# Streaming-encoder trunk on one core: x loaded in four pieces, the first weight slot in two halves, the second slot's low part made on VectorE

## The reference, cut to what matters

```python
def rmsnorm(x, g):
    xf = x.astype(jnp.float32)
    y = xf * lax.rsqrt(jnp.mean(xf * xf, axis=-1, keepdims=True) + EPS)
    return (y * g.astype(jnp.float32)).astype(x.dtype)

def stick_breaking_mixer(h, w_in, w_out):      # layer 0; w_in is 2048 x 6144
    qkv = h @ w_in
    q, k, v = jnp.split(qkv, 3, axis=-1)
    ...
    return o @ w_out

def reference(x, ...):
    for i in range(DEPTH):
        h = rmsnorm(x, norm_mix[i])
        x = x + (stick_breaking_mixer if i == 0 else mlstm_mixer)(h, ...)
        x = x + hierarchical_moe(rmsnorm(x, norm_ffn[i]), ...)
    return rmsnorm(x, norm_final)
```

## Time and profile before

| what | value |
|---|---|
| median of 3 runs | 1786.22 us (1786.12 to 1786.3) |
| the profiled execution | 1786.37 us, span 1784.6 us from first to last instruction |
| mean granted TensorE clock | 0.946 |
| TensorE busy | 1570.1 us, 88% of the span |
| VectorE busy | 731.6 us, 41% |
| ScalarE busy | 423.9 us, 24% |
| GpSimd busy | 57.7 us, 3% |
| moved by DMA | 543.79 MB, mean 305 GB/s |

### The profile page before, as it was taken

One profiled execution on the slowest core, in us unless ns is written; L12 is line 12 of the kernel. 1 busy time (PEld: TensorE's weight loads), 2 busy tenths in 40 slices (PEclk: granted clock), 3 DMA queues, 4 the chain that ended last, 5 costly groups with the idle time before them and its releaser, 6 DMA issues.

```text
span 1784.6 us, 25622 instructions
## 1 busy us (share of the span) xinstructions
PE 1570.1 (88%) x9901; PEld 1070.3 (60%) x9901; DVE 731.6 (41%) x1143; ACT 423.9 (24%) x571; POOL 57.7 (3%) x82
## 2 busy tenths in 40 slices
PE   7999999999987788778799999999998877887785
PEld 7999999887433233323287988988863333233331
DVE  4544444444322223222264756657443322222233
ACT  5344343433000000000154334334320000000002
POOL 4010000100000000000011000000000000000000
PEclk9999999999998899889899999999999998899887
DMA  8545455458999999999954465555689999999996
GB/s 270 189 146 181 148 182 166 144 212 313 394 424 425 427 424 425 425 428 424 411 170 141 144 209 168 164 194 175 225 345 426 424 425 425 427 424 425 425 427 268
DMA packets 149419, 543.79 MB, mean 305 GB/s; under 512 B 8736, under 2 KB 25456, under 8 KB 116208
## 3 DMA queue, kind: packets, MB, share of 16 engines
q1 hardware_dynamic: 148448, 541.14, 78.1%
q0 software_dynamic: 912, 1.82, 0.4%
HBM read 540.83 MB, written 2.10 MB: 304 GB/s over the span
## 4 chain that ended last, share of the span: by engine, by line
PE 58%; DMA 29%; SPq 6%; DVE 2%; ACT 2%; issue 1%; DVEq 0%; ACTq 0%
PE psum_G L663 32%; DMA ring<-in_moe_w 29%; PE psum_S L663 16%; SPq L508 6%; PE psum_A L663 6%; PE psum_T L663 3%; DVE w_lo L407 1%; ACT w_hi L403 1%; ACT h L1313 0%; DMA x<-in_x 0%; PE psum_A L670 0%; ACT squares L1147 0%; DVE x L1658 0%; DVE h L1904 0%; PE psum_T L899 0%
## 5 line engine op out<-in xcount | busy, mean ns | idle before, releaser
L663 PE MATMUL psum_A<-ring,arena 128*32 128x512 f32 x1984 | 298.5, 731 | 155.6 <-DMA ring<-in_moe_w 153.9
L407 DVE TENSOR_TENSOR w_lo<-ring,w_hi 128x2048 fp32r<-128x2048 f32 x126 | 289.2, 2298 | 289.2 <-ACT w_hi L403 285.0
L403 ACT CAST w_hi<-ring 128x2048 fp32r<-128x2048 f32 x128 | 244.2, 1908 | 244.6 <-PE psum_G L663 155.8
L663 PEld LDWEIGHTS psum_A<-ring,arena 128*32 128x32 f32 x1984 | 68.1, 122 | 331.9 <-issue 331.6
L1787 DVE COPY arena_two<-psum_A 128x512 f32<-128x512 f32 x64 | 44.3, 692 | 365.8 <-PE psum_A L663 365.4
L1817 DVE TENSOR_TENSOR x<-x,psum_S 128x512 f32<-128x512 f32 x128 | 88.0, 687 | 173.8 <-PE psum_S L663 173.8
L663 PE MATMUL psum_G<-xT_hi,w_hi 128*128 128x256 f32 x512 | 148.8, 291 | 1.1 <-DVE w_lo L407 1.1
L663 PE MATMUL psum_G<-xT_hi,w_lo 128*128 128x256 f32 x512 | 144.7, 283 | 0.0
L663 PE MATMUL psum_G<-xT_lo,w_hi 128*128 128x256 f32 x512 | 144.7, 283 | 0.0
L663 PE MATMUL psum_G<-ring,arena_two 128*32 128x512 f32 x1024 | 121.0, 614 | 22.9 <-DMA ring<-in_moe_w 22.9
L1329 ACT ACTIVATE arena<-psum_T 128x64 f32<-128x64 f32 x64 | 14.3, 224 | 500.0 <-PE psum_T L663 500.0
(11 more groups left out here) (243 smaller groups left out, 2116.3 us busy)
## 6 DMA issues: line engine op xcount, KB each, us to landing
ring<-in_moe_w SPq DMA_DIRECT2D x376, 1024.0 KB, 19.7
ring<-in_sb_w_in SPq DMA_DIRECT2D x48, 1024.0 KB, 5.1
ring<-in_ml_w_in SPq DMA_DIRECT2D x48, 1024.0 KB, 5.1
ring<-in_sb_w_out SPq DMA_DIRECT2D x16, 1024.0 KB, 4.9
ring<-in_ml_w_out SPq DMA_DIRECT2D x16, 1024.0 KB, 5.1
extra_one<-in_moe_w SPq DMA_DIRECT2D x4, 1024.0 KB, 8.6
extra_two<-in_moe_w SPq DMA_DIRECT2D x4, 1024.0 KB, 17.6
x<-in_x SPq DMA_DIRECT2D x2, 1024.0 KB, 6.0
```

Of the source, the lines that this page charges most:

```text
L403: act.copy(w_hi[:, slot_place(j), :], ring[:, slot_place(j), :]).then_inc(hi_made, 1)
L407: dve.tensor_tensor(w_lo[:, slot_place(j), :], ring[:, slot_place(j), :], w_hi[:, slot_place(j), :].bitcast(F32), ALU.subtract).then_inc(l ...
L663: return pe.matmul(dst, lhsT, rhs, start=start, stop=stop, skip_group_check=True)
```

## The change

- x comes in four loads of 512 KB: first the columns 0 to 1023 of both token blocks, then the columns 1024 to 2047 of both. TensorE waits for the first two before unit 0, and for the other two before unit 4.
- Slot 0 comes in two loads of 512 KB (k-tiles 0 and 1, then 2 and 3), with a semaphore for each half. ScalarE casts and VectorE subtracts each half by itself. TensorE starts on the first half, and waits for the second (`lo_made` 1) ahead of k-tile 2.
- The split of slot 0 moves behind unit 3 (it was behind unit 1) on ScalarE and VectorE. ScalarE casts slot 1 behind unit 4 (it was unit 3).
- In layer 0 VectorE makes the low part of slot 1, behind its unit 5, and counts it. GpSimd's split of slot 1 and the waits for it (`pool_lo_made`, the drain) are gone from layer 0; GpSimd goes from its constants straight to `load_small`. Layer 1 stays as it was.

```diff
-        x_loaded = [sem(f"x_loaded_{b}") for b in range(TB)]
+        x_loaded = [sem(f"x_loaded_{n}") for n in range(2)]
+        first_half_loaded = sem("first_half_loaded")
+        first_half_hi = sem("first_half_hi")
+        first_half_lo = sem("first_half_lo")
...
+        def first_slot(tensor, half):
+            return tensor[:, slot_place(0), half * (SLOT // 2):(half + 1) * (SLOT // 2)]
+
+        def first_slot_hi(act):
+            act.wait_ge(first_half_loaded, 16)
+            act.copy(first_slot(w_hi, 0), first_slot(ring, 0)).then_inc(first_half_hi, 1)
+            act.wait_ge(raw_loaded[0], 16)
+            act.copy(first_slot(w_hi, 1), first_slot(ring, 1)).then_inc(hi_made, 1)
+
+        def first_slot_lo(dve):
+            dve.wait_ge(first_half_hi, 1)
+            dve.tensor_tensor(first_slot(w_lo, 0), first_slot(ring, 0), first_slot(w_hi, 0).bitcast(F32),
+                              ALU.subtract).then_inc(first_half_lo, 1)
+            dve.wait_ge(hi_made, 1)
+            dve.tensor_tensor(first_slot(w_lo, 1), first_slot(ring, 1), first_slot(w_hi, 1).bitcast(F32),
+                              ALU.subtract).then_inc(lo_made, 1)
...
-            for b in range(TB):
-                sp_eng.dma_start(x[:, b, :], x_in[0, b * P:(b + 1) * P, :]).then_inc(x_loaded[b], 16)
+            for n in range(2):
+                for b in range(TB):
+                    c = slice(n * D // 2, (n + 1) * D // 2)
+                    sp_eng.dma_start(x[:, b, c], x_in[0, b * P:(b + 1) * P, c]).then_inc(x_loaded[n], 16)
+            for half in range(2):
+                sp_eng.dma_start(first_slot(ring, half).rearrange("p (k n) -> p k n", k=2),
+                                 sb_w_in[0].rearrange("(k p) n -> p k n", p=P)[:, 2 * half:2 * half + 2, 0:COLS]
+                                 ).then_inc(raw_loaded[0] if half else first_half_loaded, 16)
             for layer in (0, 1):
                 if layer == 0:
-                    mix_stream(layer, 0, range(RAW))
+                    mix_stream(layer, 0, range(1, RAW))
...
-            split_lo_one(0)
             load_small(0)
...
                 for u in range(KT // 2):
+                    if layer == 0 and u % 4 == 0:
+                        pe.wait_ge(x_loaded[u // 4], 16 * TB)
...
-                    pe.wait_ge(lo_made, mix_slot(layer, i, j) + 1)
+                    if layer == 0 and isinstance(i, int) and i == 0 and j == 0:
+                        pe.wait_ge(first_half_lo, 1)
+                    else:
+                        pe.wait_ge(lo_made, mix_slot(layer, i, j) + 1)
...
+                                    if j == 0 and kk == 2:
+                                        pe.wait_ge(lo_made, 1)
...
-                else:
-                    for b in range(TB):
-                        pe.wait_ge(x_loaded[b], 16)
...
-                    if u == 3 or (u == 1 and layer == 0):
-                        split_hi(act, layer, 0, u // 2)
+                    if layer == 0 and u == 3:
+                        first_slot_hi(act)
+                    if u == (3 if layer else 4):
+                        split_hi(act, layer, 0, 1)
...
-                    if u == 1 and layer == 0:
-                        split_lo(dve, layer, 0, 0)
-
-                dve.wait_ge(pool_lo_made, layer + 1)
-                dve.drain().then_inc(lo_made, 1)
+                    if layer == 0 and u == 3:
+                        first_slot_lo(dve)
+                    if layer == 0 and u == 5:
+                        split_lo(dve, layer, 0, 1)
+
+                if layer:
+                    dve.wait_ge(pool_lo_made, 1)
+                    dve.drain().then_inc(lo_made, 1)
```

## The result

The changed kernel takes 1791.4 us (median of 9 runs, 1790.48 to 1792.61), the kernel before 1786.12 (9 runs beside it). The ratio is 1.0029, with a 95% interval from 1.0021 to 1.0038: 5.3 us slower. That is the side to which the forecast leaned and the very top of its range (1791.4); the likeliest time was 1789.6.

A forecast was written before the change was run, and what follows sets the result against it. Slot 1's start on TensorE was taken to set the end: 2.1 us later through small loads delaying its landing, plus 1.3 for the clock, +3.4 on 1786.37, or 1789.8, less 0.15 to the median: 1789.6 us; range 1784.2 to 1791.4.

The forecast's parts named there:

- The instant that matters: When TensorE starts slot 1 and never waits again, 22.64 us before the change; moving it moves the end by as much.
- What the removed wait held back: GpSimd's small loads, without the split ahead of them, issue 18.1 us earlier, at 5.0 us, over slots 0, 1 and 2.
- I take 4.0, between the two: Delay of slot 1's landing by the small loads, 4.0 us, between 2.6 and 5.4, since queued loads fill empty places.
- The 2.5 taken for slot 0: Delay of slot 0's landing by the small loads, some 2.5 us, half of their traffic still to come.
- Cutting loads in pieces ... cost nothing: Loads in pieces and two or three more SyncE issues of 0.43 us each cost nothing, covered by the queue's backlog.
- Slot 1 lands at 18.8, starts at 24.7: Slot 1 lands at 14.8 + 4.0 us; cast, unit 5 and `w_lo` follow, so it starts 2.1 us later than before.
- The clock: TensorE, idle for 3.6 us ahead of slot 1, falls to 1.2 GHz; 1.3 us taken, up to 1.6 possible.
- What follows stays covered: Slots 2 and 3 are still ready before TensorE needs them; the slack of 2.0 us becomes 1.2.
- Full price: Rival, chance 0.14: small loads cost slot 1 5.4 us and the clock falls, 3.5 + 1.6 = +5.1 us, 1791.3.
- The clock holds: Rival, chance 0.22: as forecast but TensorE's clock doesn't fall, +2.1 us (0.7 to 3.5), 1788.3.
- Cheap small loads: Rival, chance 0.20: small loads' packets fit between others or in gaps; slot 1 starts at 20.7, time 1784.3 us.

The follow-up runs named there:

- e7: The changed kernel with only the router's four small loads early; gate weights and the rest wait for slot 1's low part: 1789.93 us, ratio 1.0021 to the kernel before.
- e10: e8 with GpSimd making slot 1's low part again, ahead of its small loads: 1786.94 us, ratio 1.0003 to the kernel before.
- e1: The changed kernel with GpSimd waiting for slot 1's low part before its small loads: 1786.11 us, ratio 1.0000 to the kernel before.
- e2: The kernel before with one edit, GpSimd issuing its small loads before its split of slot 1: 1793.04 us, ratio 1.0039 to the kernel before.
- e3: The kernel before with only x in four loads of 512 KB, TensorE waiting for all four: 1787.79 us, ratio 1.0010 to the kernel before.
- e4: e1 with VectorE making slot 1's low part behind unit 4 in place of unit 5: 1784.64 us, ratio 0.9992 to the kernel before.
- e9: e5 with slot 0 loaded, split and waited for whole: 1788.33 us, ratio 1.0011 to the kernel before.
- e5: e4 with x in two 1 MB loads, one for each half of the columns: 1784.46 us, ratio 0.9989 to the kernel before.
- e8: e5 with the split of slot 0 behind unit 2 in place of unit 3: 1784.10 us, ratio 0.9988 to the kernel before.
- e6: e5 with x in two loads of whole rows, TensorE waiting for both: 1786.28 us, ratio 0.9999 to the kernel before.

## Why the prediction was right, and where it wasn't

- **The instant that matters.** Right. Over the twelve kernels of the table slot 1's start goes from 20.2 to 29.2 us; the time less that start is 1763.3 to 1764.3 us in all of them but e7 (1761.8), where the profiled execution stands 1.2 above the median. In the profiled executions themselves the span less that start is 1761.1 to 1762.4 in all but e10 (1763.4), whose clock falls behind the start.
- **What the removed wait held back.** Right in kind, too small in size. The step "I take 4.0, between the two" failed: the idea that a deeper queue fills the places is wrong. Measured: 4.8 us of slot 1's landing (e1) and 5.8 (e2), or, counted from the landing of x, 5.5 and 5.6. The upper bound, 5.4 from slot 5's landing, was the figure to take. The 2.5 taken for slot 0 was too small by more: its second half lands 7.8 us after x in the changed kernel and 2.5 after it in e1 (slot 0 landed 2.6 after x before), so the small loads cost it 5.2 to 5.3. Slot 0's first half, for which nothing was added, landed at 16.1 and not 10.9, and TensorE started slot 0 at 18.5 where 15 to 16 was the sign named. The Trainium skill (DMA: Bandwidth & Descriptors, the anatomy of one DMA) gives a load from GpSimd 2.0 us plus its bytes at 436 GB/s, and an estimate by its second term is 1.0 us for the 0.44 MB of small loads. The traces disagree: 5.5 to 5.6 us.
- **"Cutting loads in pieces ... cost nothing".** Wrong. The backlog was there, but x in four pieces moves at 329 GB/s in place of 414 and is complete 1.4 us later (e3; 1.5 to 2.1 in e4, e7 and e1), and slot 1 with it. Slot 0 in halves did cost nothing (e1). The extra issues weren't the reason: SyncE was through with them at 7.4 us, before the slots' data was due.
- **Slot 1 lands at 18.8, starts at 24.7.** It landed at 21.7: 2.9 more, 1.4 for x and 1.5 for the small loads (5.5 in place of 4.0). The 5.9 us from landing to start measured 5.8, with unit 5 in the middle of it, as worked out; e4 shows that this order alone costs 1.4.
- **The clock.** 1.3 us were taken; it cost nothing here. The fall came, but behind the idle time ahead of slot 0 (4.8 us), where slot 1 was late anyway; ahead of slot 1 TensorE idled for 1.3 us and not 3.6, since slot 0 came late itself. The term missed upward while the other two missed downward, so the sum, +3.4 against +5.3, looks better than its parts. Where the fall is on the path it costs 0.4 (e2), 1.1 (e7), 1.2 (e9) and 1.5 us (e10) in the profiled executions. At the low clock a matmul begins every 0.21 us, not 0.24.
- **What follows stays covered.** Right: no new wait behind slot 1.
- **The rivals.** *Full price* came nearest, for its first reason and not its second: the small loads at 5.4 were there, the clock's 1.6 were replaced by the slower x. That its 1791.3 was met so closely is luck. *The clock holds* was right that the clock costs nothing, and too low because it took 4.0 for the small loads and nothing for x. *Cheap small loads* is refuted by e1.
- **The size of the effect.** The forecast gave 0.63 to a difference of less than 3.6 us and 0.34 to one above it, slower; 5.3 us is the latter. The range holds the result only by its upper end, which stands on the full price.

Left open: why the router's four loads take most of the price (4.6 of 5.6 us); and whether the pieces of x are slow by their number or by their 4 KB runs (e5, between the two, points to both). The short rows themselves weren't varied.

## What to carry to other kernels

When a wait is taken out, list every DMA that stood behind it in that engine's program and ask what it will now meet; a load of 0.3 MB in rows of 16 and 128 bytes can hold up megabytes. Find the price by the late landing of a big load that once ran beside it, and take that figure whole, not a share of it: 5.4 was read, 5.5 came. The same edit with one wait put back, and the second split ahead of a unit that isn't urgent, turned +5.3 us into -1.6 (e4, an interval that touches no change), and two better cuts into -2.2 (e8). Count such a price from the landing of what goes ahead in the queue: the landing of x alone moved by 0.8 us between profiles.

## What the runs showed of the hardware that wasn't expected

- x in four pieces of 512 KB with 4 KB runs came at 315 to 331 GB/s in the stretch 5:9 us (changed kernel, e3, e1 and e4 alike; 299 in e7), in two loads of 1 MB with 4 KB runs at 384 to 389 (e5, e8, e9, e10), in two with whole rows of 8 KB at 409 to 414 (before, e6), and at 401 with GpSimd issuing its small loads beside them (e2).
- An idle TensorE of 4.8 us (changed kernel), 3.0 (e9) and 2.2 us (e10) was followed by a granted clock of 0.50 for about 3.4 us; with 5.8 (e2) and 6.6 us (e7) the clock fell while it was still idle and stood at 0.50 for about 6.8. After 1.9 us (e3, ahead of slot 0) and after 1.3 us (e1, ahead of slot 1) it stayed at 1.00. In the changed kernel the fall cost nothing, since slot 1 became ready 1.5 us after slot 0 had ended. The first idle stretch, ahead of the turning, isn't counted here: the profile gives 1.00 for it, though the first eight transposes take 1.94 us and the last eight 1.04.
